# An encoder's routed experts: wider groups of weight columns, and weights cut five tiles ahead in place of three

## What is computed

```
D_MODEL, D_FF, N_EXPERTS, TOP_K = 1024, 3584, 8, 2

def _swiglu(h, w_gate_up, w_down):
    gu = h @ w_gate_up                       # (tokens, 1024) @ (1024, 7168)
    g, u = gu[..., :D_FF], gu[..., D_FF:]
    return (jax.nn.silu(g) * u) @ w_down     # @ (3584, 1024)

def _moe(h, router, w_gate_up, w_down):
    logits = (h @ router).astype(jnp.float32)
    top_v, top_i = lax.top_k(logits, TOP_K)
    gates = jax.nn.softmax(top_v, axis=-1)
    ...
    for e in range(N_EXPERTS):
        y = y + gate_full[..., e:e + 1] * _swiglu(h, w_gate_up[e], w_down[e])
```

## Times and profile before

| | us |
|---|---|
| median of 3 runs | 1522.73 |
| the runs | 1520.2, 1522.73, 1609.3 |
| span of the profiled execution | 1520.2 |
| that execution's own time | 1522.17 |

### The profile page before, as it was taken

How to read it: one execution, slowest core, us unless ns; L and a number is a source line. 1 busy time by engine, 2 the same in 40 slices (tenths; PEclk the granted TensorE clock), 3 DMA queues, 4 the chain that set the end, 5 groups by cost and what they waited for, 6 DMA issues and landing times.

```text
span 1520.2 us, 19543 instructions
## 1 busy us (share of the span) xinstructions
PE 1481.3 (97%) x7678; PEld 1208.7 (80%) x7678; DVE 1158.3 (76%) x1021; ACT 991.1 (65%) x869; POOL 132.2 (9%) x137
## 2 busy tenths in 40 slices
PE   8999999999989999999999999999999999999996
PEld 6888888899969987888777788777888777888774
DVE  5555445454565456899899988899898999898997
ACT  5544434343453337777798777888776888776986
POOL 0000000006034314000000200000100000000000
PEclk9999999999999999999999999999999999999999
DMA  9655555567516653899999999999999999999996
GB/s 333 214 170 190 168 192 171 189 192 224 194 57 213 206 185 126 329 356 355 366 405 417 398 407 405 395 408 415 399 408 403 395 408 415 399 404 408 393 391 220
DMA packets 151056, 468.26 MB, mean 308 GB/s; under 512 B 9856, under 2 KB 15872, under 8 KB 138416
## 3 DMA queue, kind: packets, MB, share of 16 engines
q1 hardware_dynamic: 144784, 453.93, 79.8%
q0 software_dynamic: 2816, 9.96, 2.3%
q10 hardware_dynamic: 3360, 3.06, 0.7%
HBM read 459.55 MB, written 7.37 MB: 307 GB/s over the span
## 4 chain that ended last, share of the span: by engine, by line
PE 79%; DVE 13%; ACT 3%; DMA 1%; SPq 1%; issue 1%; DVEq 0%; ACTq 0%
DVE wlo L418 9%; PE bS L437 6%; PE bS L438 6%; PE bS L436 6%; PE bY L436 6%; PE bY L438 6%; PE bY L437 6%; PE bG L436 4%; PE bG L438 4%; PE bU L436 4%; PE bG L437 4%; PE bU L438 4%; PE bU L437 4%; DVE wlo_more L418 2%; ACT whi L412 2%
## 5 line engine op out<-in xcount | busy, mean ns | idle before, releaser
L418 DVE TENSOR_TENSOR wlo<-raw,whi 128x2048 fp32r<-128x2048 f32 x364 | 827.2, 2296 | 179.6 <-ACT whi L412 178.4
L412 ACT ACTIVATE whi<-raw 128x2048 fp32r<-128x2048 f32 x364 | 692.3, 1915 | 262.1 <-PE bS L438 118.2
L418 DVE TENSOR_TENSOR wlo_more<-raw_more,whi 128x2048 fp32r<-128x2048 f32 x60 | 136.4, 2288 | 10.7 <-ACT whi L412 10.6
L412 ACT ACTIVATE whi<-raw_more 128x2048 fp32r<-128x2048 f32 x60 | 114.5, 1914 | 28.0 <-DMA raw_more<-in_m_w_gate_up_dram 8.4
L1086 PE MATMUL bY<-whi,hTh 128*128 128x512 f32 x224 | 91.5, 408 | 6.9 <-DVE wlo L418 4.9
L436 PE MATMUL bY<-whi,hTh 128*128 128x512 f32 x224 | 89.8, 401 | 0.0
L437 PE MATMUL bY<-whi,hTl 128*128 128x512 f32 x224 | 89.1, 398 | 0.0
L437 PE MATMUL bS<-whi,eTl 128*128 128x512 f32 x192 | 76.4, 398 | 0.0
L436 PE MATMUL bS<-whi,eTh 128*128 128x512 f32 x192 | 76.4, 398 | 0.0
L1086 PE MATMUL bS<-whi,eTh 128*128 128x512 f32 x192 | 76.3, 398 | 0.0
L1087 PE MATMUL bY<-wlo,hTh 128*128 128x512 f32 x184 | 73.2, 398 | 0.0
(11 more groups left out here) (536 smaller groups left out, 3336.4 us busy)
## 6 DMA issues: line engine op xcount, KB each, us to landing
raw<-in_m_w_gate_up_dram SPq DMA_DIRECT2D x184, 1024.0 KB, 14.5
raw<-in_m_w_down_dram SPq DMA_DIRECT2D x90, 1024.0 KB, 14.4
raw_more<-in_m_w_gate_up_dram SPq DMA_DIRECT2D x40, 1024.0 KB, 14.6
raw<-in_b_w_in_dram SPq DMA_DIRECT2D x36, 1024.0 KB, 5.1
raw<-in_f_w_gate_up_dram SPq DMA_DIRECT2D x28, 1024.0 KB, 5.2
raw_more<-in_m_w_down_dram SPq DMA_DIRECT2D x20, 1024.0 KB, 14.2
raw<-in_f_w_down_dram SPq DMA_DIRECT2D x14, 1024.0 KB, 5.0
raw<-in_a_w_out_dram SPq DMA_DIRECT2D x4, 1024.0 KB, 16.8
```

Source lines behind the costliest of these rows:

```text
L412: nc.scalar.activation(whi[:, h], raw_of(r), ACT.Copy).then_inc(hi_done, 1)
L418: nc.vector.tensor_tensor(wlo_of(r), raw_of(r), whi[:, h].bitcast(F32), ALU.subtract).then_inc(lo_done, 1)
```

## The change

It acts on the expert layer and on one constant.

- w_gate_up is taken as GROUPS = 3 groups of 2048 columns and one of 1024. A tile t < NARROW = 24 is now 128 rows x 2048 columns, so each row gives 8 KB in one piece in place of 4 KB. Tiles 24 to 27 are 256 rows x 1024 columns (4 KB pieces in place of 2 KB).
- A tile feeds four PSUM banks at once (G, S0, S1, U), and all four are done only in the group's last tile (7, 15, 23). The next group begins in the same four banks: `bank_free` makes PE wait, bank by bank, for SiLU or copy (or, from group 2 on, for the product with up). A new semaphore `gu_psum` tells when each bank's sums stand. Gate slabs are parked in `parked` (7 slabs, in the space of the low hidden part); group 1 ends with gates 4 to 6 and up 0, group 2 is up 1 to 4, the last is up 5 and 6.
- The slabs are turned at tiles 17, 24, 25, 27, 29, 31 and 33 instead of in step with the passes.
- High parts get six buffers from tile T_LATE on (two further ones in memory that is dead by then: `hn` and the final norm's gain), and ACT and DVE cut LEAD = 5 tiles ahead.
- Since its place is in use, the final norm's gain is loaded by SP behind the last expert load, once the last tile that uses that buffer is used.
- The last item takes its first 6 down tiles as whole rows and only the last 8 as halves.

```diff
-            if t < SINGLE:
-                g, r = divmod(t, 8)
-                part, q = divmod(r, 4)
-                c = part * FF + g * 1024
-                return gate_up[q * 256:q * 256 + 256, c:c + 1024].rearrange("(k p) n -> p k n", p=P)
+            if t < NARROW:
+                g, kb = divmod(t, KD)
+                return gate_up[kb * P:kb * P + P, g * 2048:g * 2048 + 2048]
             if t < DOWN:
...
+                q = t - NARROW
+                return gate_up[q * 256:q * 256 + 256, GROUPS * 2048:2 * FF].rearrange("(k p) n -> p k n", p=P)
...
+        T_LATE = -(-(T_MOE + HI + 1) // HI) * HI
+        def hi_slot(t):
+            return t % HI if t < T_LATE else (0, HI, HI + 1, 1, 2, 3)[(t - T_LATE) % (HI + 2)]
+        def hi_free(t, item):
+            if isinstance(item, int) and in_order(t, item) > T_LATE:
+                return used_count(t, item, HI + 2)
+            return used_count(t, item, HI)
...
+        gate_up_banks = G, S0, S1, U
+        def column_sums(engine, n, g, s):
+            if s == (3 if g < GROUPS else 1):
+                engine.wait_ge(tile_used, count(n, FFN_TILES, T_MOE + (KD * g + KD if g < GROUPS else DOWN)))
+            else:
+                engine.wait_ge(gu_psum, count(n, 10, 3 * g + s + 1))
...
+            last_of_gain = max(t for t in range(T_MOE + E * FFN_TILES) if t >= T_LATE and hi_slot(t) == HI + 1)
+            sp.wait_ge(tile_used, last_of_gain + 1)
+            sp.dma_start(*CONST[C_GAIN4]).then_inc(c_in[C_GAIN4], 16)
...
+                def bank_free(g, s):
+                    if g == 1:
+                        pe.wait_ge(gate_copied, count(k, SLABS, s + 1))
+                    if g == 2 and s < 3:
+                        pe.wait_ge(gate_copied, count(k, SLABS, s + 5))
+                    if g == 2 and s == 3:
+                        pe.wait_ge(up_copied, count(k, SLABS, 1))
+                    if g == 3:
+                        pe.wait_ge(up_copied, count(k, SLABS, s + 2))
...
+                turned = {18: 0, 25: 1, 26: 2, 28: 3, 30: 4, 32: 5, 34: 6}
+                for t in range(FFN_TILES):
+                    ahead(t)
+                    if t == 3:
+                        amid(0)
+                    if t in (7, 15):
+                        for j in range(4) if t == 7 else range(4, SLABS):
+                            copy_gate(j)
+                    if t in (15, 23, 27):
+                        copy_ups((t - 7) // KD if t < 27 else 3)
+                    if t in turned:
+                        slab_silu(turned[t])
+                    if t - 1 in turned:
+                        slab_hi(turned[t - 1])
```

More of the change, by code:

```diff
@@ L155, in encoder @@
         phase = top[0]
+        top[0] = at_hn
+        whi_late = place("whi_late", [2048], F32R)
+        assert top[0] == phase
         top[0] = at_hn
@@ new lines, in full_item @@
+                for t in range(DOWN):
+                    gate_up_product(t)
+                    if t in turns:
+                        turn(turns[t])
+                    if t in (3, 11, 25):
+                        amid(t // KD)
+                before_down()
+                for t in range(DOWN, FFN_TILES):
+                    pe.wait_ge(ht_lo, count(k, SLABS, PAIRS0 + (t - DOWN) // 2 + 1))
+                    down_product(t)
+                    if t in turns:
+                        turn(turns[t])
+                    if t == DOWN + 5:
@@ new lines, in gate_up_product @@
+                def gate_up_product(t):
+                    tile_ready(T_MOE + t, n)
+                    for s, blk, kb, stop in blocks_of(t, False):
+                        if t < KD:
+                            tokens_ready(n, kb, s)
+                        if kb == 0:
+                            bank_free(t // KD, s)
+                        w = wblk_backward(T_MOE + t, blk, n)
+                        pe.matmul(backward(gate_up_banks[s], 0, 512), eTh[:, kb], w[0], start=kb == 0, stop=False)
+                        mm = pe.matmul(backward(gate_up_banks[s], 0, 512), eTh[:, kb], w[1], start=False, stop=stop)
+                        if stop and s < (3 if t < NARROW else 1):
+                            mm.then_inc(gu_psum, 1)
+                    mm.then_inc(tile_used, 1)
@@ L1115, in half_item @@
-                pe.wait_ge(gate_copied, count(k, SLABS, 2 * PAIRS))
-                product(SINGLE, eTh, (G,))
-                product(SINGLE + 1, eTh, (G,))
-                turn(2 * PAIRS - 2)
-                amid(PAIRS)
-                product(SINGLE + 2, eTh, (U,))
-                turn(2 * PAIRS - 1)
-                product(SINGLE + 3, eTh, (U,))
+                turns = {17: 0, 24: 1, 25: 2, 27: 3, 29: 4, 31: 5, 33: 6}
+                for t in range(DOWN):
+                    gate_up_product(t)
+                    if t in turns:
+                        turn(turns[t])
+                    if t in (3, 11, 25):
+                        amid(t // KD)
@@ L1123, in half_item @@
                 before_down()
                 for t in range(DOWN, FFN_TILES):
-                    slab = (t - DOWN) % DT if by_half else (t - DOWN) // 2
-                    if not by_half or t < DOWN + DT:
+                    slab = (t - DOWN) // 2
+                    if by_half and t >= DOWN + LAST_WIDE:
+                        slab = LAST_WIDE // 2 + (t - DOWN - LAST_WIDE) % LAST_HALF
+                    if not by_half or t < DOWN + LAST_WIDE + LAST_HALF:
                         pe.wait_ge(jt_lo, count(k, SLABS, slab + 1))
-                    product(t, hTh, (Y0, Y1))
@@ L1129, in half_item @@
-                    if t == DOWN + (0 if by_half else 2):
-                        turn(SLABS - 1)
+                    down_product(t)
+                    if t in turns:
+                        turn(turns[t])
                     if by_half and t in (DOWN + 7, DOWN + 9):
```

440 lines of the change are left out of this document (173 added, 267 removed).

## The result

| | us | ratio to the kernel before |
|---|---|---|
| before, median | 1523.36 | |
| after, median of 4 runs | 1541.74 (1538.84 to 1547.33) | 1.0126 (95% interval 1.0093 to 1.0158) |
| after, the profiled execution | 1547.33, span 1545.5 | |

One of the four runs of before (1609.3) was a slow one, and the ratio leaves it out. The change made the kernel 18 us slower. The forecast was 1511.5 with a range up to 1528.

What follows compares the result with a forecast made beforehand. PE, DVE and saturated DMA were all taken as near their limit. Half items 7.5, full items 0.6 and last item 3.1 gave 11.2 off the 1520.2 span: 1509.0, plus 2.5 for the median, 1511.5; range 1499 to 1528.

Steps and rivals of the forecast that it cites:

- Wider pieces: Expert tile loads: 8 KB pieces at 422 GB/s lower DMA's floor for a pair from 222.4 to 217.7 us.
- a second bound that lies on top of the first: Item pairs: saturated DMA takes the same 222.4 us for 84 tiles as the engines do.
- Six buffers and a lead of five: Half items: DVE starts about two tiles richer and stops being the bound; up to 7.9 us to be had.
- Four banks at once: Half items: waits at tiles 8, 16, 24 and behind cost about 5.1 us, giving 97.5; full items no stall.
- Full items: Items 2, 4, 6: no stall at the banks, deeper lead takes 122.4 to 122.2 us, 0.6 in all.
- Last item: Last half item: PE's part 94.7 plus 4 of stalls, 98.7 against 101.8 us, a gain of 3.1.
- The gain loaded late: Final norm's gain, loaded behind SP's last expert load: hidden by at least 4 us, no cost.
- B: Tiles 8, 16, 24: the lead costs the ring its depth, 2.5 to 5 us a pair; 1518 to 1528; chance 0.2.
- C: Every boundary, full items too: ACT late, slower, median 1561 us; half the lateness about 1535; chance 0.1.
- A: Half items: stalls hide and DMA is the bound, 95.5 us each; whole 1502.4, median 1505; chance 0.17.
- D: Tile loads: bytes a piece do not matter, DMA's floor stays 222.4 us; time 1520 to 1523; chance 0.08.
- three signs of being wrong: Full items over 123 us, DMA share below 1.00 in the pairs, or half items under 96 or over 100.

Runs made afterwards that it cites:

- (9): Kernel before with half the bytes of each expert tile from item 1 on, engines doing as many elements; 1518.42 us, ratio 0.9980.
- (8): Kernel after with half the bytes of each expert tile from item 1 on, engines doing as many elements; 1535.64 us, ratio 1.0096.
- (10): Kernel after, full items' SiLUs, products and cuts two tiles earlier, half items' bank copies behind cuts of tiles 10, 17, 24; 1540.27 us, ratio 1.0120.
- (11): (10) with every slab's SiLU, product and cut three tiles earlier, copies behind cuts of tiles 10, 17, 25 and 29; 1532.04 us, ratio 1.0072.
- (13): (11) with DVE's routing steps three tiles earlier in half items and two earlier in full items; 1514.46 us, ratio 0.9946.
- (5): Kernel after with the half items' bank-freeing copies two cuts earlier in ACT's order; 1539.63 us, ratio 1.0103.
- (15): Kernel before with six high buffers, lead of five only over item borders and in half items, half the bytes; 1499.27 us, ratio 0.9841.

## Why the prediction was wrong, point by point

- **Wider pieces.** The rate was right: tiles 13 to 20 of half item 3, with 8 KB pieces, landed one every 2.48 to 2.50, at 425 GB/s in the window below (422 in the earlier trace rows). By the Trainium skill ("DMA: Bandwidth & Descriptors", section Bandwidth) the size of the whole transfer counts, the same 1 MB before and after; by that rule nothing would have changed. The rows here speak against it: 387, 410 and 422 GB/s for 2, 4 and 8 KB pieces at one size of transfer. What the rate is worth was wrong: I read DMA share 1.02 as a second bound, "a second bound that lies on top of the first". Run (9) shows before 3.2 us faster with half its bytes, and the last item's 3.3 is all of that. The share says that the queues had work, not that anybody waited for it.

```profile
985.00:1000.00 15.00, 14.83 (x57) 11.79 (x58) 15.00 (x7) 12.81 (x10) 0.00 (x0) 0.89 1.01 425
```

- **Six buffers and a lead of five.** Right where nothing but cuts is queued: tiles 0 to 7 gain 1.5. That the loads do not set before's half items was right too (9), and DVE is busy for 97.2 of their 100.0. That they would fall to PE's floor was right of the old groups (93.8 with the loads away, against my 92.1 and 92.7 by the new table).
- **Four banks at once: the step that failed.** I put 1.5 + 1.5 + 0.6 at tiles 8, 16 and 24 and 1 to 1.5 behind it, 5.1 in all; measured are 106.5 - 92.7 = 13.8 in item 3, above even my upper bound of 12.3. Three things are to be told apart.
  - The landing. I priced the cut ahead of the copies by ACT's own pace (1.91 against PE's 1.87), and the three waits at 3.6 together; they are 2.0, 3.1 and 1.8, 6.9. At tile 8 the price was near, for tile 12 had landed at 982.6 and PE was through tile 7 at 983.2. At tile 16 the tile to be cut had not landed. I had averaged the ring over a pair (a swing of 5 tiles); inside a half item PE takes the first 16 tiles at 1.87 where one lands every 2.49, so that the landed tiles fall from 9 to 4 there, below the lead of 5. In the last item they fall to 3, and the wait is 7.3.
  - The clock, for which the sum had no term. Behind the three waits it was at 0.50 for 13.6 us, 6.8 us lost, the other half of the 13.8.
  - Engines behind engines. Halving the bytes took only 4.1 of the 13.8 (8). PE's idle time in item 3 stayed at 6.9; a wait of 4.4 at tile 24 took the place of the landings, for the first slab's product behind DVE's low parts. I had seen one such place ("stands behind DVE's cut of tile 30") and given it 1 to 1.5; in (10) it cost 3.6 of idle time. The row numbers are a third, and cost nothing in after itself, where tiles 28 to 34 take the 21.4 of PE alone: they came up in (11), when the others were gone.
- **Full items.** Right: 122.2. But item 0 costs 2.0, which I had at 0 (137.3 with a lead of three). At tiles 16 and 24 PE waits 0.9 and 0.4 for DVE's product of gate and up, which stands behind deeper cuts; that DVE's routing work in this item is what makes it late was not tested alone.
- **Last item.** Forecast 98.7, measured 108.1: tile 16 alone takes 11.0, by the same mechanism with three landed tiles. With the order mended it takes 99.9 (11) and 100.2 (13).
- **The gain loaded late.** Right. It was issued at 1524.1, 12 us ahead of its first reader at 1536.5, and nobody waited for it.
- **Rivals.** B had the mechanism, word for word ("PE must not begin tile 8, 16 or 24 before tile 12, 20 or 28 has landed and been cut"), with a price of 2.5 to 5 a pair, taken from the full items' side; it costs the half item 5.3 to 6.5 against before and the full item nothing. That the stalls themselves let the ring fill up again fits the counts: after's full items begin with six landed tiles, those of (5) that took 126.2 and 125.5 with five and four. C named the places (every boundary) and gave 1535 for half its lateness; it was the nearest number, but by ACT's pace, which is what made ACT late at tile 8 alone. A and D start from a bound by DMA that was not there. The range ended at B's upper part and left C out, so 1541.7 lies above it; two of my three signs of being wrong came (half items over 100, a DMA share below 1.00 in the full items).

## What to carry to other kernels

A lead is a position in an in-order program, so whatever stands behind it inherits it: for each thing that PE waits for on another engine, list what stands ahead of it there, and ask when *that* can run (has its tile landed, is its buffer free, is the engine itself slower than PE). Give the lead only to stretches where nothing that is waited for is queued, such as the border between items, and take it back ahead of each hand-over. And a busy DMA share is no bound: halving the bytes with the engines' work kept shows in one run what the loads cost in that order of the engines. Where it gives back little, as in (8), look which wait has taken their place. And count a wait of PE with what comes behind it: here the low clock cost as much again.

## What the runs showed of the hardware that I had not expected

After most of its waits TensorE ran at half its clock for a stretch. Behind the wait of 3.11 us the products follow at 0.23 us from 1005.07 to 1006.32 and at 0.43 from 1006.63 on, the step from 2.4 to 1.2 GHz. The three stretches of half item 3 (columns of the earlier trace rows):

```profile
985.96:989.36 3.40, 3.40 (x10) 2.60 (x9) 3.40 (x3) 3.32 (x4) 0.00 (x0) 0.50 1.01 426
1006.45:1009.85 3.40, 3.40 (x10) 2.75 (x9) 1.95 (x2) 3.40 (x2) 0.00 (x0) 0.50 1.00 408
1026.93:1033.73 6.80, 6.80 (x25) 6.04 (x24) 5.77 (x3) 3.85 (x3) 0.00 (x0) 0.50 1.02 423
```

PE was busy through all of them, so its busy share does not show them. Behind nine of the twelve border waits of after's half items the clock fell. Eight times it did so 0.2 to 1.4 us after PE had begun again; in the wait of 7.26 us it fell at 1460.4, 3.1 us after the wait had begun, and stayed down for 10.2. A wait of 1.98 us (item 1, tile 8) was not followed by a fall, one of 1.95 (item 3, tile 8) was. The mean clock differs between after's executions (0.984 to 0.991), and the longer ones have the lower clock; their times lie within 8.5 us where 19 of before lie within 6. Only one execution of each kernel has a trace, so that other falls are what spreads them is not shown.

Half the bytes of a tile did not halve DMA's share: it was 0.70 to 0.76 in half items and 0.63 to 0.64 in full ones, from 0.99 to 1.03, at about half the GB/s. The size of the pieces does not tell: the new groups' pieces shrank from 8 to 4 KB in (8), the old groups' gate and up tiles loaded half as many pieces of the same size in (15), and both have some 71 us of DMA time in a half item (0.70 x 102.4 and 0.76 x 93.8). The cause stays open.
